# Scan of a hybrid decoder step: the samples' B and C spread over the partitions by a store and a broadcast load instead of diagonals and products with ones

## The chip, the cores and the metric

The kernel runs on one core of a Trainium2 chip. The metric is the device time of one execution in microseconds; the time before is the median of three runs. The profile is that of one execution.

## The reference, cut to what matters

One inference step of a two-layer decoder for a prompt of 1024 tokens and, beside it, 8 samples of one token each. Layer 1 is a Mamba-2 mixer with 8 groups of 4 heads (64 channels a head, 128 state elements). For the prompt it is a scan over 8 chunks of 128 tokens. For the samples, chunk length 1, it is per sample, group and head:

```
new_state = state * exp(dt * a) + outer(x * dt, B)     # (64, 128) per head
y         = new_state @ C
```

B and C are vectors of 128 elements for each sample and group. Each has to be multiplied, along the free axis, with every one of the group's 256 channels, which lie in the partitions (2 halves of 128).

## The kernel before, in words

`mamba_groups` runs the layer's input projection and the scan in one loop. All work is float32; a weight matrix comes as a high and a low part, and each product with it is made in three passes.

- In a turn of the loop (`part(g, nx)` on each engine), TensorE makes the 18 tiles of group nx = g + 1's projection (units 0 to 5 of three tiles: x, x, B, C, z, z; `tile`, line 2992) and between them, in `slot(g, k)` for k = 0 to 8, the scan of group g: `turn` (lines 3006 and 3007) turns chunk k to rows, `scan` (lines 3018 to 3026) makes the products of chunk k - 1. There is a slot behind tiles 0 to 5 and 7 to 9 of the turn. Behind slot 2 stands tile 0 of unit 1, which needs `w_low` of that unit from GpSimd (`split_low`, line 234).
- The last group has no next one. Its `closing` interleaves the slots with the first tiles of the output projection (`nxt`, class `ProjectOdd`), whose input `gated_raw` SyncE loads back from a scratch in DRAM (line 3503), ScalarE casts (line 3535) and VectorE subtracts (line 3539).
- The samples' part: GpSimd builds `dg`, the identity times the column B (later C) of each sample (`diagonals`, line 2859). TensorE multiplies it with ones (`spread`, line 3036), which leaves B of 8 samples in all partitions, in PSUM banks 6 and 7: B in slot 2, C in slot 5. VectorE multiplies from PSUM: `outer` (line 3337, behind chunk 1) and `sample_y` (line 3345, behind chunk 4).
- GpSimd, in its own order: first diagonals, six small stores of conv rows (lines 2877, 2878), then per chunk x_decayed (2922), x_d (2930), and from chunk 1 on the decay of the state (2937). In between come the decay of the sample states (2945, behind chunk 1), `w_low` of unit 1, behind chunk 3 the second diagonals and the additions to the sample states (2957), `w_low` of unit 2, and the eight stores of the sample states (2868, behind chunk 4).
- SyncE, in its own order: the spread decay sums (2 MB, line 2820), the sample states (8 loads of 128 KB, line 2826), then the weights of the units (line 220), each behind a wait for an earlier `w_low`.

Each engine runs its list strictly in order; the order is written out by hand, and engines wait for each other by semaphores that count.

Of the kernel before, what the change touches and what calls it, by code (L numbers as in the profile page):

```python
# [7 lines left out]
F32 = mybir.dt.float32  # L8
# [8 lines left out]
P = 128  # L17
# [2683 lines left out]
def mamba_groups(B, nxt, steps):  # L2701
# [29 lines left out]
    dg = B.take("diagonals_sb", [P, NS, P])  # L2731
# [13 lines left out]
    cst = gz[0:PAD + NS, 0:2, :].rearrange("p n (j c) -> p (n j) c", j=2)  # L2745
    sst = xd[:, 0, :].rearrange("p (c n) -> p c n", c=2)
    B.g_scratch = nc.dram_tensor("gated_scratch", (16, P, TOK), F32, kind="Internal").ap()
# [9 lines left out]
             "square_sums", "rstd", "gated_scaled", "gated_turned", "gated_stored_col", "diagonal", "spread", "outer",  # L2757
             "sample_state", "sample_gated", "sample_sum", "conv_rows_turned", "conv_rows_kept", "state_turned",
             "state_rows", "pad_set", "sample_scaled", "sample_decayed", "sample_mean", "column_half")
    S = {n: B.sem(n) for n in names}  # L2760
    s_bc, s_st, s_sto = B.sem("spread_loaded"), B.sem("sample_ssm_loaded"), B.sem("sample_ssm_stored")
# [37 lines left out]

    with nc.Block() as block:  # L2800
        @block.sync
        def _(sp):
# [13 lines left out]
            def part(g, nx, more):  # L2816
                if g is not None:
# [3 lines left out]
                                                ap=[[0, P], [SEQ, HPG], [1, SEQ]])).then_inc(s_bc, 16)  # L2821
                    sp.wait_ge(s_sto, g * (16 * NS))
# [5 lines left out]
                if nx is not None:  # L2828
                    for e in range(1, 6):
                        load_unit(nx, e)  # L2830
                if more:
                    load_unit(nx + 1, 0)
                if nx is None:
# [10 lines left out]
                    sp.wait_ge(S["diagonal"], G * 2)  # L2844
# [10 lines left out]
        def _(pool):  # L2855
            def diagonals(j):

                for b in range(0, NS, 4):
                    ins = nc.gpsimd.tensor_tensor(dg[:, b:b + 4], B.ident[:].unsqueeze(1).to_broadcast([P, 4, P]),
                                                  post[:, j, SEQ + b:SEQ + b + 4].unsqueeze(2).to_broadcast([P, 4, P]), ALU.mult)  # L2860
                ins.then_inc(S["diagonal"], 1)

# [39 lines left out]
            def part(g, nx, more):  # L2902
                splits = [] if nx is None else [1, 2, 3]
                if g is not None:

                    pool.wait_ge(S["conv_out"], g * 4 + 4)
                    pool.wait_ge(S["sample_gated"], g)
                    diagonals(2)
                for k in range(9):
# [7 lines left out]
                    if k < NBLK:  # L2917
# [16 lines left out]
                        if n >= 1:  # L2934
# [5 lines left out]
                                                    ALU.mult).then_inc(S["state_decayed"], 1)  # L2940
                    if k == (1 if nx is not None else 2):
# [9 lines left out]
                    if k == 3:  # L2951
# [3 lines left out]
                        diagonals(3)  # L2955
# [25 lines left out]
        def _(pe):  # L2981
# [15 lines left out]
            def turn(g, n):  # L2997

                if n == 0:
                    pe.wait_ge(S["conv_out"], g * 4 + 4)  # L3000
                    pe.wait_ge(S["gated_stored_col"], g * 8)
# [732 lines left out]
```

## Time and profile before

| what | value |
|---|---|
| median of 3 runs | 3382.21 us (3376.72 to 3386.57) |
| the profiled execution | 3382.08 us, span 3380.3 us |
| mean granted TensorE clock | 0.973 of full speed |
| TensorE busy (matmul) | 3218.8 us, 95% of the span |
| VectorE, ScalarE, GpSimd busy | 45%, 34%, 36% |
| the scan's loop with its opening and closing | about 1620 to 2490 us of the span |

In the rows below PE is TensorE, PEld its weight load, DVE VectorE, ACT ScalarE, POOL GpSimd, SP SyncE; SPq is SyncE's queue of issues. A row of the timeline gives the start and the duration in us, the engine, the line, the operation, output and inputs, and how many were merged (x4); in brackets stands the idle time of the engine ahead of it and what ended it. A granted clock of 1.00 is full speed.

### The profile page before, as it was taken

To read this page: it belongs to the slowest core of one execution; us is meant where nothing else is said; L and a number is where in the kernel's file an instruction comes from. 1 tells how busy PE (TensorE), PEld (TensorE's weight loads), DVE (VectorE), ACT (ScalarE), POOL (GpSimd) and SP (SyncE) were. 2 spreads that over 40 slices of the span, in tenths; PEclk is the share of its full clock that TensorE was granted. 3 is DMA by queue.
4 is the path that set the end of the run, shared out by engine and by line. 5 is a ranking of instruction groups with operands and counts; after the bars stand their busy time and mean duration, and the time that the engine had idled before them with its cause. 6 is when DMAs were issued, how large, how long until landed. Compare 5 with 4: busy or idle time off the path is not lost. (4 is left out here: it accounts for less than half of the span.)

```text
span 3380.3 us, 56747 instructions
## 1 busy us (share of the span) xinstructions
PE 3218.8 (95%) x20604; PEld 3043.0 (90%) x20604; DVE 1524.9 (45%) x2687; ACT 1143.0 (34%) x2132; POOL 1207.2 (36%) x890
## 2 busy tenths in 40 slices
PE   7889988889999999999999999999899999999998
PEld 6569984669999999999998899989889999999997
DVE  3699994533212212122666767776732212121222
ACT  3512214643312212133444555554532312122222
POOL 2206844413222221213356555566533121212222
PEclk9979999889999999999999999999999999999998
DMA  4218646033111111112322223321431111111111
GB/s 137 55 32 138 193 167 223 10 132 58 51 44 45 48 44 49 44 50 77 100 76 68 85 83 98 98 81 58 158 133 50 44 44 50 44 50 43 49 45 69
DMA packets 344008, 263.90 MB, mean 78 GB/s; under 512 B 52134, under 2 KB 308150, under 8 KB 341910
## 3 DMA queue, kind: packets, MB, share of 16 engines
q1 hardware_dynamic: 327926, 232.18, 23.0%
q0 software_dynamic: 8192, 19.13, 1.7%
q10 hardware_dynamic: 7776, 11.09, 1.5%
q8 instruction: 69, 1.13, 0.1%
q14 instruction: 45, 0.37, 0.0%
HBM read 219.43 MB, written 44.76 MB: 78 GB/s over the span
## 5 line engine op out<-in xcount | busy, mean ns | idle before, releaser
L234 POOL TENSOR_TENSOR w_low_sb<-w_loaded_sb,w_high_sb 128x1024 fp32r<-128x1024 f32 (+1 forms) x278 | 569.3, 2055 | 1541.0 <-ACT w_high_sb L226 1517.2
L252 PE MATMUL psum<-act_high_sb,w_high_sb 128*128 128x344 f32 (+1 forms) x2400 | 770.5, 321 | 9.5 <-PEq L2800 4.6
L252 PE MATMUL psum<-act_low_sb,w_high_sb 128*128 128x344 f32 (+1 forms) x2400 | 768.8, 320 | 0.0
L252 PE MATMUL psum<-act_high_sb,w_low_sb 128*128 128x344 f32 (+1 forms) x2400 | 768.6, 320 | 0.0
L252 PE MATMUL psum<-second_high_sb,w_high_sb 128*128 128x344 f32 x1728 | 553.3, 320 | 0.5 <-PEq L2391 0.5
L252 PE MATMUL psum<-second_low_sb,w_high_sb 128*128 128x344 f32 x1728 | 551.9, 319 | 0.0
L252 PE MATMUL psum<-second_high_sb,w_low_sb 128*128 128x344 f32 x1728 | 551.9, 319 | 0.0
L252 PEld LDWEIGHTS psum<-act_high_sb,w_high_sb 128*128 128x128 f32 (+1 forms) x2400 | 451.6, 188 | 10.3 <-issue 9.0
L252 PEld LDWEIGHTS psum<-act_low_sb,w_high_sb 128*128 128x128 f32 (+1 forms) x2400 | 451.6, 188 | 0.7 <-issue 0.3
L252 PEld LDWEIGHTS psum<-act_high_sb,w_low_sb 128*128 128x128 f32 (+1 forms) x2400 | 451.9, 188 | 0.4
L226 ACT CAST w_high_sb<-w_loaded_sb 128x1024 fp32r<-128x1024 f32 (+1 forms) x230 | 239.5, 1042 | 519.9 <-PE psum L252 498.6
L2992 PE MATMUL psum<-act_high_sb,w_high_sb 128*128 128x344 f32 x1104 | 368.4, 334 | 11.0 <-POOL w_low_sb L234 10.8
L756 DVE TENSOR_TENSOR x_sb<-x_sb,psum 128x344 f32 (+1 forms) x192 | 98.4, 513 | 600.7 <-PE psum L252 600.7
L2992 PE MATMUL psum<-act_high_sb,w_low_sb 128*128 128x344 f32 x1104 | 353.2, 320 | 0.0
L2992 PE MATMUL psum<-act_low_sb,w_high_sb 128*128 128x344 f32 x1104 | 353.0, 320 | 0.0
L252 PEld LDWEIGHTS psum<-second_high_sb,w_high_sb 128*128 128x128 f32 x1728 | 324.5, 188 | 0.8 <-issue 0.8
L252 PEld LDWEIGHTS psum<-second_high_sb,w_low_sb 128*128 128x128 f32 x1728 | 324.8, 188 | 0.0
L252 PEld LDWEIGHTS psum<-second_low_sb,w_high_sb 128*128 128x128 f32 x1728 | 324.5, 188 | 0.0
L688 ACT ACTIVATE relu_square_sb<-relu_sb 128x344 f32<-128x344 f32 x192 | 94.5, 492 | 447.0 <-DVE relu_sb L741 447.0
L741 DVE SCALAR_TENSOR_TENSOR relu_sb<-psum,rstd_sb 128x344 f32<-128x344 f32 x192 | 99.2, 517 | 293.8 <-PE psum L252 269.6
L2992 PEld LDWEIGHTS psum<-act_high_sb,w_high_sb 128*128 128x128 f32 x1104 | 208.3, 189 | 21.3 <-issue 20.1
L2992 PEld LDWEIGHTS psum<-act_low_sb,w_high_sb 128*128 128x128 f32 x1104 | 208.1, 188 | 2.6 <-issue 1.7
(434 smaller groups left out, 4758.7 us busy)
## 6 DMA issues: line engine op xcount, KB each, us to landing
w_loaded_sb<-in_w_up SPq DMA_DIRECT2D x64, 512.0 KB, 4.1
w_loaded_sb<-in_w_down SPq DMA_DIRECT2D x64, 512.0 KB, 3.6
w_loaded_sb<-in_w_in_odd SPq DMA_DIRECT2D x48, 512.0 KB, 4.0
key_pages_sb<-in_cache_k SPq DMA_DIRECT2D x64, 256.0 KB, 3.1
ecay_sum_spread_sb<-decay_sum_scratch SPq DMA_DIRECT2D x8, 2048.0 KB, 9.8
w_loaded_sb<-in_w_in_even SPq DMA_DIRECT2D x28, 512.0 KB, 4.0
value_pages_sb<-in_cache_v SPq DMA_DIRECT2D x52, 256.0 KB, 5.2
gated_scratch<-gated_sb POOLq DMA_DIRECT2D x8, 1032.0 KB, 4.4
```

What stands on the lines that cost most here:

```text
L226: self.nc.scalar.copy(self.wh[:, par, :, 0:width], self.wf[:, par, :, 0:width]).then_inc(self.s_w_high, 1)
L234: ins = self.nc.gpsimd.tensor_tensor(self.wl[:, par, k, 0:width], self.wf[:, par, k, 0:width], self.wh[:, par, k, 0:width].bitcast(F32), A ...
L252: ins = nc.tensor.matmul(out, w[:, par, k, 0:width], a[:, k, cols], start=n == 0, stop=n == 3 * KT - 1)
L688: nc.scalar.activation(self.sq[:, s, :], self.relu[:, s, :], ACT.Square).then_inc(self.s_square, 1)
L741: nc.vector.scalar_tensor_tensor(out=self.relu[:, s, :], in0=B.tile(self.par(e), t), scalar=0.0, in1=self.norm.rstd[:, tcols(t)], op0=ALU.max,
L756: nc.vector.tensor_tensor(xs, xs, B.tile(self.par(e), t), ALU.add).then_inc(B.s_tile_free, 1)
L2992: ins = nc.tensor.matmul(B.psum[:, t, 0:TT], w[:, par(e), k, :], a[:, k, tcols(t)], start=m == 0, stop=m == 3 * KT - 1)
```

## The change

The samples' B and C of a group are turned to rows by TensorE (two transposes of 8 columns, at the beginning of slot 0, into PSUM bank 6), copied to SBUF by VectorE (8 rows of 1 KB, kept in a part of the gated rows that chunk 2 uses later), stored to a scratch in DRAM by SyncE, and loaded from there to all 128 partitions by GpSimd's queue: B behind chunk 0, C behind chunk 3, each 128 times the same 8 pieces of 512 bytes. VectorE reads them from SBUF. The diagonals and the products with ones go. On SyncE the weights of units 1 and 2 now go out ahead of a wait for the rows, then the store, then the eight loads of the sample states.

```diff
-    dg = B.take("diagonals_sb", [P, NS, P])
+    spr = B.take("sample_b_or_c_sb", [P, NS, P])
...
+    bcr = gz[0:NS, 2, :].rearrange("b (i n) -> b i n", i=2)
...
+    B.bc_scratch = nc.dram_tensor("sample_b_c_scratch", (G, NS, 2, P), F32, kind="Internal").ap()
...
+    def load_spread(eng, g, i):
+
+        eng.wait_ge(s_bcs, g * 16 + 16)
+        B.hold(eng)
+        eng.dma_start(spr[:], bass.AP(tensor=B.bc_scratch.tensor, offset=g * (2 * NS * P) + i * P,
+                                      ap=[[0, P], [2 * P, NS], [1, P]])).then_inc(s_spr[i], 16)
...
# SyncE, part(g, nx), behind the load of the decay sums
+                    if nx is not None:
+                        load_unit(nx, 1)
+                        load_unit(nx, 2)
+                    sp.wait_ge(S["sample_rows"], g + 1)
+                    B.hold(sp)
+                    sp.dma_start(B.bc_scratch[bass.ds(g, 1)].rearrange("o b i n -> b (o i) n"), bcr).then_inc(s_bcs, 16)
                     sp.wait_ge(s_sto, g * (16 * NS))
                     sp.wait_ge(S["sample_gated"], g)
...
-                    for e in range(1, 6):
+                    for e in range(1 if g is None else 3, 6):
...
-                    sp.wait_ge(S["diagonal"], G * 2)
+                    sp.wait_ge(s_spr[1], 16 * G)
...
# GpSimd
-            def diagonals(j):
-
-                for b in range(0, NS, 4):
-                    ins = nc.gpsimd.tensor_tensor(dg[:, b:b + 4], B.ident[:].unsqueeze(1).to_broadcast([P, 4, P]),
-                                                  post[:, j, SEQ + b:SEQ + b + 4].unsqueeze(2).to_broadcast([P, 4, P]), ALU.mult)
-                ins.then_inc(S["diagonal"], 1)
...
-                if g is not None:
-
-                    pool.wait_ge(S["conv_out"], g * 4 + 4)
-                    pool.wait_ge(S["sample_gated"], g)
-                    diagonals(2)
...
+                    if k == 0:
+                        pool.wait_ge(S["sample_gated"], g)
+                        load_spread(pool, g, 0)
...
-                        diagonals(3)
+                        load_spread(pool, g, 1)
...
# TensorE, turn(g, 0)
+                    pe.wait_ge(S["sample_mean"], g)
+                    for i in range(2):
+                        ins = nc.tensor.transpose(B.psum[0:NS, 6, i * P:(i + 1) * P], post[:, 2 + i, SEQ:TOK], B.ident[:])
+                    ins.then_inc(S["sample_turned"], 1)
...
-            def spread(g, m):
-
-                await_group(pe, S["diagonal"], g, 2, m + 1)
-                if m == 0:
-                    pe.wait_ge(S["state_rows"], g)
-                    pe.wait_ge(S["sample_scaled"], g)
-                for a in range(2):
-                    ins = nc.tensor.matmul(B.psum[:, 6 + a, :], B.ones[:],
-                                           dg[:, 4 * a:4 * a + 4, :].rearrange("p b n -> p (b n)"), start=True, stop=True)
-                ins.then_inc(S["spread"], 1)
...
-                if k == 2:
-                    spread(g, 0)
-                if k == 5:
-                    spread(g, 1)
...
# VectorE: gate(g, 2), outer(g), sample_y(g), part(g, nx)
+                if n == 2:
+                    dve.wait_ge(s_bcs, g * 16 + 16)
...
-                await_group(dve, S["spread"], g, 2, 1)
+                dve.wait_ge(s_spr[0], g * 16 + 16)
                 for c in range(2):
-                    ins = nc.vector.tensor_tensor(tmp[:, c], B.psum[:, 6:8, :].rearrange("p a (b n) -> p (a b) n", b=4),
+                    ins = nc.vector.tensor_tensor(tmp[:, c], spr[:],
                                                   small(0)[:, c, :].unsqueeze(2).to_broadcast([P, NS, P]), ALU.mult)
...
-                await_group(dve, S["spread"], g, 2, 2)
+                dve.wait_ge(s_spr[1], g * 16 + 16)
...
+                    dve.wait_ge(S["sample_turned"], g + 1)
+                    dve.wait_ge(S["gated_turned"], g * 8)
+                    nc.vector.tensor_copy(bcr, B.psum[0:NS, 6, 0:2 * P].rearrange("b (i n) -> b i n", i=2)).then_inc(S["sample_rows"], 1)
```

## Rows read from the trace of the kernel before

**Rows 1.** Stretches view, 100 us of the loop: busy us per engine, clock, DMA
```profile
2000.00:2100.00 100.00, 96.03 (x621) 91.08 (x619) 70.60 (x110) 52.30 (x125) 56.91 (x64) 1.00 0.28 86
```

**Rows 2.** Timeline of TensorE, turn g = 1
```profile
1790.59 0.60 PE L3069 MATMUL psum<-ident_sb,conv_in_sb 128*11 128x128 f32 x4
...
1808.16 0.59 PE L3026 MATMUL psum<-x_decayed_sb,x_b_rows_sb 128*128 128x256 f32 x2
...
1808.59 1.88 PE L3036 MATMUL psum<-diagonals_sb,ones_sb 128*128 128x512 f32 x4
...
1811.51 0.42 PE L2992 MATMUL psum<-act_high_sb,w_high_sb 128*128 128x344 f32 x1 [1.04 <-POOL w_low_sb L234]
...
1831.81 0.70 PE L3026 MATMUL psum<-x_decayed_sb,x_b_rows_sb 128*128 128x256 f32 x2 [0.87 <-POOL x_decayed_sb L2922]
...
1848.46 0.38 PE L3018 MATMUL psum<-ident_sb,z_sb 128*128 128x128 f32 x2
```

**Rows 3.** Timeline, GpSimd, the same turn
```profile
1801.73 0.78 POOL L2922 TENSOR_TENSOR x_decayed_sb<-x_b_rows_sb,decay_to_end_sb 128x256 f32<-128x256 f32 x1 [0.76 <-ACT x_b_rows_sb L3186]
...
1804.20 4.07 POOL L2945 TENSOR_TENSOR ample_ssm_state_sb<-ample_ssm_state_sb,_channel_values_sb 128x512 f32<-128x512 f32 x4
...
1819.96 0.80 POOL L2937 TENSOR_TENSOR n_state_decayed_sb<-scan_state_sb,chunk_decay_sb 128x256 f32<-128x256 f32 x1
...
1820.72 2.03 POOL L2859 TENSOR_TENSOR diagonals_sb<-ident_sb,conv_out_sb 128x512 f32<-128x512 f32 x2
...
1822.72 5.65 POOL L2957 TENSOR_TENSOR ample_ssm_state_sb<-ample_ssm_state_sb,conv_sum_sb 128x512 f32<-128x512 f32 x4
```

**Rows 4.** Timeline, VectorE, the same turn
```profile
1813.42 2.36 DVE L3337 TENSOR_TENSOR conv_sum_sb<-psum,sample_small_sb 128x1024 f32<-128x1024 f32 x2
...
1827.22 1.43 DVE L3324 TENSOR_TENSOR y_sb<-y_sb,x_d_sb 128x256 f32<-128x256 f32 x1
...
1847.68 0.42 DVE L3326 TENSOR_TENSOR gated_rows_sb<-y_sb,psum 128x256 f32<-128x256 f32 x1
```

**Rows 5.** The groups by form, TensorE
```profile
L3036 PE MATMUL psum<-diagonals_sb,ones_sb 128*128 128x512 f32 x64 | 30.1, 592 | 0.0
```

**Rows 6.** Single lines (ns min/median/max) and the state loads' landing
```profile
L982 POOL DMA_DIRECT2D index_pages_sb<-in_cache_idx_k x32: 535/535/717, 83.2 to 141.9; - x32
...
L2868 POOL DMA_DIRECT2D out_ssm_sample<-ample_ssm_state_sb x64: 710/713/798, 1733.7 to 2443.1; - x64
...
L2826 SPq DMA_DIRECT2D ample_ssm_state_sb<-in_state_ssm x64: 372/446/3139, 1674.8 to 2382.4; - x64
...
DMA to landing us min/median/max: 4.0/7.1/8.5
...
L3382 DVE SCALAR_TENSOR_TENSOR conv_sum_sb<-conv_in_sb,conv_weights_sb,conv_sum_sb x96: 1283/1285/2160, 1641.8 to 2385.4; 128x1024 f32<-128x1024 f32 x96
```

**Rows 7.** TensorE's timeline at two idle times, and stretches there
```profile
615.12 1.86 PE L1898 MATMUL psum<-qkv_sb 64*128 64x512 f32 x4 [2.06 <-DVE minus_row_max_sb L1963]
...
615.40:618.80 3.40, 3.40 (x13) 1.76 (x12) 2.95 (x7) 1.03 (x2) 0.73 (x1) 0.50 0.00 0
...
571.35 1.13 PE L1898 MATMUL psum<-qkv_sb 64*128 64x512 f32 x4 [1.34 <-DVE minus_row_max_sb L1968]
...
568.00:575.00 7.00, 5.66 (x56) 3.08 (x60) 3.96 (x15) 3.52 (x8) 0.73 (x1) 1.00 0.01 2
```

**Rows 8.** Timeline of the last group's beginning, and gated_raw's landing
```profile
2387.89 4.82 SPq L3503 DMA_DIRECT2D gated_raw_sb<-gated_scratch  x8
...
2394.89 2.66 POOL L2859 TENSOR_TENSOR diagonals_sb<-ident_sb,conv_out_sb 128x512 f32<-128x512 f32 x2
...
2396.36 3.90 ACT L3535 CAST act_high_sb<-gated_raw_sb 128x1032 fp32r<-128x1032 f32 x4
...
2401.89 1.22 PE L3026 MATMUL psum<-x_decayed_sb,x_b_rows_sb 128*128 128x256 f32 x2 [2.77 <-POOL x_decayed_sb L2922]
...
DMA to landing us min/median/max: 5.3/6.9/8.7
```

More of the change, by code:

```diff
@@ L2756, in mamba_groups @@
              "exps", "cb_masked", "scores", "x_dt", "x_decayed", "x_d", "state_decayed", "state", "gated",
-             "square_sums", "rstd", "gated_scaled", "gated_turned", "gated_stored_col", "diagonal", "spread", "outer",
+             "square_sums", "rstd", "gated_scaled", "gated_turned", "gated_stored_col", "sample_turned", "sample_rows", "outer",
              "sample_state", "sample_gated", "sample_sum", "conv_rows_turned", "conv_rows_kept", "state_turned",
@@ L2760, in mamba_groups @@
     S = {n: B.sem(n) for n in names}
+    s_bcs, s_spr = B.sem("sample_b_c_stored"), [B.sem("sample_b_loaded"), B.sem("sample_c_loaded")]
     s_bc, s_st, s_sto = B.sem("spread_loaded"), B.sem("sample_ssm_loaded"), B.sem("sample_ssm_stored")
@@ L3053, in sample_sum @@
                 pe.wait_ge(S["sample_gated"], g + 1)
+                pe.wait_ge(S["sample_rows"], g + 1)
                 nc.tensor.matmul(B.psum[:, 6, 0:16], B.ones[:], sml[:, 3, :], start=True, stop=True).then_inc(S["sample_sum"], 1)
@@ L3090, in turn_state @@
                 await_group(pe, S["state"], g, NBLK, NBLK)
+                pe.wait_ge(S["state_rows"], g)
                 for j in range(2):
@@ L3341, in sample_y @@
             def sample_y(g):
-                await_group(dve, S["spread"], g, 2, 2)
+                dve.wait_ge(s_spr[1], g * 16 + 16)
                 dve.wait_ge(S["sample_state"], g + 1)
                 for c in range(2):
-                    step(nc.vector.tensor_tensor(tmp[:, c], B.psum[:, 6:8, :].rearrange("p a (b n) -> p (a b) n", b=4),
+                    step(nc.vector.tensor_tensor(tmp[:, c], spr[:],
                                                  st[:, :, c, :], ALU.mult))
```

## The prediction

> **What bounds the kernel now.** I read the busy times first: 100 us of the scan's loop hold 96.0 us of TensorE at full clock, and no other engine comes near [rows 1]. So work taken off TensorE can pay in full, 4 us in 100 are waits, and what counts is where they stand. Next came the timeline of one turn of the loop at the places where the products with ones stand, for TensorE and for GpSimd, then VectorE's, and last SyncE's order. All times are of the turn g = 1; the other six turns with a next group look alike.
>
> At the end of slot 2 TensorE makes the first spread and then still stands 1.04 us for w_low of the next unit, from GpSimd, until 1811.51. At slot 5 it stands 0.87 us for x_decayed of chunk 4, from GpSimd again, and makes the second spread behind it [rows 2]. So at both places where work is taken from TensorE, GpSimd is the later of the two. At slot 7 no wait is seen, but gated of chunk 5 ends at 1848.10 on VectorE (1847.68 + 0.42), 0.36 us ahead of the scan that needs it, L3018 at 1848.46 [rows 2, 4].
>
> **What is taken from TensorE.** A spread is four passes in 1.88 us, each of 0.59, so they follow at (1.88 - 0.59) / 3 = 0.43 us and cost 1.72 us; 16 of them (64 passes) 27.5 us [rows 2, 5]. Added are two turns of eight columns per group. The nearest row is that of the four turns of the conv rows, 0.60 us [rows 2]: 0.15 each, 0.3 us per group, 2.4 in all. Net 25.1 us, if nothing else ended the waits. The two turns are free in slot 0, as TensorE waits for the first scores in slot 1 anyway, and VectorE's copy of eight rows (0.4 us by its forms of 256 columns [rows 4]) falls in its wait for the first rows.
>
> **The GpSimd side, first half.** The first diagonals (as long as the second, 2.03 us [rows 3]) stand ahead of stores and a wait for ScalarE; nothing is won by their going. What comes in is the issue of a load of 128 x 8 pieces of 512 bytes, behind x_d of chunk 0. Its landing is hidden: it goes out near 1802 and is used at 1813.42 [rows 4], and the slowest of the state loads lands in 8.5 us [rows 6]. Its issue isn't hidden. GpSimd's issues take 0.54 us for one piece in each of 128 partitions and 0.71 for two pieces [rows 6]. By the count of pieces eight would be 0.54 + 7 x 0.17 = 1.73; if only the form counts, 0.71. I take 1.2, about the middle, as eight pieces are far from both. Of it 0.76 us fall in the wait ahead of x_decayed of chunk 1 [rows 3]; 0.44 us push the decay of the states and w_low behind it: TensorE gets w_low 0.44 us later (0 to 0.97), though it comes there 1.7 us earlier.
>
> The states of the samples are now loaded behind the rows instead of a half turn ahead. The copy is done near 1795.7 (the first chunk's turns end there), SyncE's store is issued by 1796.2, the eight loads at 0.45 us each (median of 64 issues) by 1799.8 (the last one from 1799.4 on). Behind the 2 MB load they took 4.0 us to land at the least and 7.1 in the median; now that load is long done, so I take 4.0: 1803.4 for the last. The other end is 1806.5. GpSimd wants them at 1804.20 + 0.44 [rows 3, 6]. I cost it at nothing; at the other end w_low is 1.9 us later still, and each us of it costs 7 in seven turns.
>
> **The clock.** TensorE is now done with slot 2 at 1808.75 (1808.16 + 0.59) and gets w_low at 1811.5 + 0.44: it idles 3.2 us where it idled 1.04. An idle time of 2.06 us ahead of 615.12 is followed by 3.4 us at a granted clock of 0.50, the lower of the two levels (1.2 of 2.4 GHz), with TensorE busy throughout; 1.34 us ahead of 571.35 leave it at 1.00 [rows 7]. I found no idle time of 2 us or more, entered at full clock, without such a fall. So I expect a fall in each turn, of which some 3.2 us lie in work at half rate: 1.6 us lost. Slot 3 starts 0.44 + 1.6 = 2.0 us late.
>
> **Second half of the turn.** Chunk 3 goes through all engines 2.0 us late, up to GpSimd's decay of the state at 1819.96. Then the diagonals (2.03) give way to the second issue (1.2): the additions start 2.0 - 2.03 + 1.2 = 1.2 us late [rows 3], and so do w_low, x_decayed of chunk 4 and VectorE's gate and sample_y. TensorE waits for x_decayed, then saves the spread: 1.2 - 1.7 = 0.5 us early at slot 6. But VectorE's chain from sample_y through gate 5 is 1.2 us late and a little more, as its products read SBUF on both sides instead of PSUM: 1.285 us by the nearest form, undisturbed, for 1.18 (2.36 / 2) [rows 4, 6]; I take 0.2 us for the two. Gated of chunk 5 comes at 1849.5, so TensorE, there 0.5 us early, waits 1.6 us and goes on 1.15 us late. The slack of VectorE ahead of chunk 7 gives 0.25 back by slot 8 (estimated). Rest: 0.9 us later per turn, 7 turns: +6.3 us. With an issue of 0.71 it is about 0 per turn, with 1.73 it is +2.0.
>
> A y + x_d of 256 columns takes 1.43 us at 1827.22, with GpSimd's additions (1822.72 to 1828.37) under way, and a form of as many columns with a PSUM operand 0.42 [rows 3, 4]: two SBUF inputs can be held up. The Trainium skill, page "SBUF — State Buffer", section "Who interferes with whom", has it as a rule: a VectorE instruction with two SBUF inputs contends with a GpSimd instruction that reads SBUF, and one blocks the other whole. The trace agrees. By it outer and sample_y, now with two SBUF inputs, would be open to blocks of up to one addition each (5.65 / 4 = 1.4 us), 0.9 us per turn would become up to 2.3, and the sum up to +12; I keep 0.2, since in the trace GpSimd waits during the one and issues stores during the other.
>
> **The last group.** There SyncE's order changes most: the loads of gated_raw, issued from 2387.89 on, now stand behind the wait for the sample's rows and eight state loads. The rows exist at about 2390, so gated_raw goes out from 2394.2 on, 6.3 us later (0.6 us for the store, eight loads at 0.45). Before, its landing (5.3 us at the least) left 3.2 us until the first cast at 2396.36; now the casts start about 2.5 us later. A cast is 1.0 us (3.90 / 4), the low part 1.3 by the form of 1024 columns, so the first pair is there at 2401.2. Against it, GpSimd loses 2.66 us of diagonals ahead of x_decayed of chunk 0, for which TensorE waited 2.77 us until 2401.89 [rows 6, 8]. Together TensorE opens the unit, then at 2402.55, some 1.0 us earlier, and saves two spreads (3.4 us), as other engines wait for TensorE there: -4.3 us (from -6 to +1).
>
> **Sum.** +6.3 - 4.3 = +2.0 us on the profiled execution's own 3382.1, which lies on the median of the three runs (3382.2): 3384 us.
>
> **Rivals.** (a) TensorE's work counts in full: -25.1, 3357 us. For it speaks only how busy TensorE is; against it the waits at both places. 4%. (b) The clock does not fall at slot 2 (the idle time ahead of 571.35 is its support). The turn then loses 1.6 less: additions 0.4 us early, -0.7 per turn, 7 x -0.7 - 4.3 = -9.2, 3373 us; with an issue of 0.71, -1.6 per turn, 3366 us. 20% for faster. (c) Slower: the 1.6 us for which TensorE waits at slot 7 let the clock fall a second time. It decides somewhere between 1.34 us (no fall) and 2.06 (fall) [rows 7]; each fall costs 1.6, 7 of them 11.2: 3395 us. With an issue of 1.73 as well (each 0.1 us of issue costs 1.4 us in seven turns): 3402. (d) Slower too: the state loads land at the late end, 1.9 x 7 = 13 us: 3397 us; it decides from 1806 on. (c) and (d) together 33%. (e) gated_raw comes later than worked out: up to +5 in the last group, 3389, within the forecast. The forecast with (e): 43%.
>
> A difference of 0.3%, 10 us, is about what a measurement of this kernel can tell from no change. Faster 0.24, same 0.43, slower 0.33. The likeliest case alone spans 3376 to 3392 (issue 0.71 to 1.73 with one fall); the range takes in (b), (c) and (d): 3364 to 3404 us. It leaves out (a), and (c) and (d) at once.
>
> The Trainium skill, page "DMA: Bandwidth & Descriptors", section "Anatomy of one DMA", would give the landing of 512 KB an estimated 3.2 us, hidden here too; no run here shows it yet.
>
> **What the profile after would show.** L3036 gone, two turns of 8 columns in slot 0; two GpSimd issues per group, near 1.2 us each; TensorE's wait for w_low behind slot 2 grown from 1.0 to about 3 us, with a granted clock of 0.50 behind it; the wait for x_decayed kept; a new wait of 1.6 us at L3018 of slot 7 for gated; no wait of GpSimd for the states; in the last group, later casts of gated_raw. Wrong would make it: an issue over 2 us, states that land well after 1804, a clock that stays at 1.00, or a turn in which VectorE is not the last at slot 7.

## The result, and the profile after

The kernel after takes 3427.9 us (median of four runs, 3426.35 to 3429.79) against 3381.0 us for the kernel before on the same chip: a ratio of 1.0135, 95% interval 1.0122 to 1.0148. The change makes it 47 us slower. The forecast was 3384 us, and its range ended at 3404.

First the same 100 us of the loop as in [rows 1] (columns as there):

```profile
2000.00:2100.00 100.00, 89.52 (x572) 86.62 (x570) 70.22 (x108) 47.70 (x111) 50.03 (x58) 0.95 0.29 91
```

TensorE is busy for 89.5 us instead of 96.0, and the clock's mean is 0.95. The turns of the loop show where the time is. The turn of [rows 2 to 4] lasted 99.55 us (1790.59 to 1890.14); its counterpart, from the first row below to the last, lasts 105.12. All seven grew, to between 103.4 and 108.2, 40.7 us in all. What lies ahead of them grew by 1.3 us, the last group and all behind it by 5.6.

TensorE's timeline of that turn (start, duration, in brackets the idle time and what ended it):

```profile
1797.49 0.60 PE L3066 MATMUL psum<-ident_sb,conv_in_sb 128*11 128x128 f32 x4
...
1818.43 0.42 PE L2999 MATMUL psum<-act_high_sb,w_high_sb 128*128 128x344 f32 x1 [2.79 <-POOL w_low_sb L234]
...
1841.68 0.66 PE L3029 MATMUL psum<-ident_sb,z_sb 128*128 128x128 f32 x2 [4.50 <-DVE gated_rows_sb L3326]
...
1902.61 0.60 PE L3066 MATMUL psum<-ident_sb,conv_in_sb 128*11 128x128 f32 x4
```

The first wait was forecast (3.2 us; it is 2.79). The second one, 4.50 us at the beginning of slot 5, for `gated` of chunk 3, was not. Where it comes from is seen on GpSimd and on VectorE. GpSimd:

```profile
1807.82 0.97 POOL L2807 DMA_DIRECT2D sample_b_or_c_sb<-sample_b_c_scratch  x1
...
1829.18 0.95 POOL L2807 DMA_DIRECT2D sample_b_or_c_sb<-sample_b_c_scratch  x1
1830.15 4.98 POOL L2964 TENSOR_TENSOR ample_ssm_state_sb<-ample_ssm_state_sb,conv_sum_sb 128x512 f32<-128x512 f32 x4
1835.08 2.50 POOL L234 TENSOR_TENSOR w_low_sb<-w_loaded_sb,w_high_sb 128x512 fp32r<-128x512 f32 x2
1837.55 0.60 POOL L2926 TENSOR_TENSOR x_decayed_sb<-x_b_rows_sb,decay_to_end_sb 128x256 f32<-128x256 f32 x1
1838.12 0.78 POOL L2934 TENSOR_TENSOR x_d_sb<-x_b_rows_sb,d_skip_sb 128x256 f32<-128x256 f32 x1
```

VectorE:

```profile
1831.90 6.54 DVE L3296 TENSOR_TENSOR x_dt_sb<-x_b_rows_sb,dt_rows_sb 128x256 f32<-128x256 f32 x1 [0.70 <-ACT x_b_rows_sb L3184]
1838.57 0.88 DVE L3303 TENSOR_TENSOR ecay_sum_spread_sb<-ecay_sum_spread_sb,cb_masked_sb 128x512 f32<-128x512 f32 x1
...
1841.16 0.42 DVE L3326 TENSOR_TENSOR gated_rows_sb<-y_sb,psum 128x256 f32<-128x256 f32 x1
```

At this place the kernel before had:

```profile
1823.42 0.85 DVE L3298 TENSOR_TENSOR x_dt_sb<-x_b_rows_sb,dt_rows_sb 128x256 f32<-128x256 f32 x1 [0.70 <-ACT x_b_rows_sb L3186]
```

`x_dt` of chunk 4, a product of 128 x 256 that takes 0.43 us elsewhere and 0.85 at this place before, lasts 6.54 us. It is ready to run 1.75 us behind the beginning of the additions. Behind the issue GpSimd works without a pause: four additions, two pieces of `w_low` (1.25 us each), x_decayed and x_d of chunk 4. x_dt ends at 1838.44, 0.29 us behind the end of x_decayed (1838.15), so it was let in only there, between x_decayed and x_d. GpSimd itself isn't slowed. `scores` and then `gated` of chunk 3 stand behind it in VectorE's order, TensorE waits for the latter. It is so in each of the seven turns, 6.54 to 7.42 us. The line's own row (ns minimum/median/maximum of all 64) and that of the issues:

```profile
L3296 DVE TENSOR_TENSOR x_dt_sb<-x_b_rows_sb,dt_rows_sb x64: 424/426/7417, 1700.8 to 2509.3; 128x256 f32<-128x256 f32 x64
...
L2807 POOL DMA_DIRECT2D sample_b_or_c_sb<-sample_b_c_scratch x16: 937/955/985, 1702.7 to 2474.0; - x16
```

TensorE's two falls of the clock in this turn, behind slot 2 and at slot 5 (stretch, its length, busy us of TensorE, its weight loads, VectorE, ScalarE and GpSimd, granted clock, DMA share, GB/s):

```profile
1818.40:1823.20 4.80, 4.76 (x20) 4.77 (x21) 3.88 (x5) 0.00 (x0) 1.80 (x3) 0.64 0.41 109
...
1841.68:1844.90 3.22, 3.22 (x13) 3.04 (x14) 1.41 (x3) 2.79 (x9) 3.22 (x5) 0.50 0.52 163
1844.90:1846.95 2.05, 2.05 (x8) 1.87 (x7) 0.95 (x3) 0.82 (x1) 2.03 (x4) 0.50 0.62 192
```

The second fall costs more than the first: TensorE works for 5.27 us (3.22 + 2.05) at 0.50.

The waits of TensorE, summed over the execution:

```profile
PE psum L3029 <- DVE gated_rows_sb L3326: 34.5, 8, 5.4
...
PE psum L2999 <- POOL w_low_sb L234: 23.0, 14, 2.8
```

And the last group, SyncE, ScalarE, VectorE and TensorE, for [rows 8]:

```profile
2432.70 4.11 SPq L2842 DMA_DIRECT2D ample_ssm_state_sb<-in_state_ssm  x8
2436.91 4.37 SPq L3506 DMA_DIRECT2D gated_raw_sb<-gated_scratch  x8
...
2442.86 2.00 ACT L3538 CAST act_high_sb<-gated_raw_sb 128x1032 fp32r<-128x1032 f32 x2 [4.38 <-DMA gated_raw_sb<-gated_scratch]
...
2463.12 4.01 DVE L3337 TENSOR_TENSOR conv_sum_sb<-sample_b_or_c_sb,sample_small_sb 128x1024 f32<-128x1024 f32 x2
...
2469.93 0.62 PE L3570 MATMUL psum<-act_high_sb,w_high_sb 128*128 128x344 f32 x1 [5.37 <-DVE x_sb L3583]
```

Its turn begins at 2429.67, 42.02 us later than before. The casts of gated_raw (2396.36 before) are 46.5 us later, so 4.5 us late in the turn. `outer`, 2.36 us in every other turn, takes 4.01: here it runs beside the decay of the sample states.

### The profile page after: what moved, and what is told of

The parts are those of the page before. It is cut to its first block and busy times, and to the rows that moved or that the text cites. A ratio compares the mean times of both kernels' runs of the same rounds, so it can differ in the third digit from the quotient of the medians.

```text
span 3427.9 us, 56729 instructions
## 1 busy us (share of the span) xinstructions
PE 3216.9 (94%) x20556; PEld 3057.9 (89%) x20556; DVE 1559.3 (45%) x2695; ACT 1143.3 (33%) x2132; POOL 1183.6 (35%) x874
```

## The experiments

Sixteen kernels were run. "x_dt(4)" is x_dt of chunk 4. A product is "held" where VectorE's row for it is longer than it is undisturbed; a "boundary" is the place between two GpSimd instructions that follow each other without a pause. Ratios are against the kernel before, run on the same chip, with 95% intervals; the runs were spread over several chips, so compare by the ratios.

**1. GpSimd waits for x_dt(4) ahead of the additions.** Theory A: the place within GpSimd's row of work decides. B: the load of C does. C: the clock's fall at slot 2 is the root. To kernel after:

```diff
                         load_spread(pool, g, 1)
+                        await_group(pool, S["x_dt"], g, NBLK, 5)
```

> The kernel after, in which GpSimd waits for VectorE's x_dt of chunk 4 before it begins the four additions to the sample states. Theory A (a product with two SBUF inputs is held through GpSimd's chain of additions and w_low when it comes within the chain): x_dt of chunk 4 takes 0.43 us instead of 6.54, the additions begin about 2.2 us later, x_decayed of chunk 4 is done near 2.7 us later than before and TensorE waits for it in slot 5, some 1.4 us per turn less than it waited for gated of chunk 3: about 3418 us (from 3428). Theory B (what holds x_dt is the load of C, issued by GpSimd just ahead): x_dt stays over 3 us though GpSimd stands, and the time rises by 2 us per turn, to about 3442.

3410.4 us, 1.0079 (1.0062 to 1.0096), below what either gave. x_dt(4) takes 0.43 us. GpSimd stood idle for 2.29 us while the load was landing; `scores` (4), asked for 0.04 us behind the beginning of the additions, ran at the first boundary (1.79 us). TensorE now waits 17.8 us in all for x_decayed, at most 2.5. The hold is what costs, and with idle time between issue and additions it does not come; the run does not separate A from B.

**2. Kernel before, second diagonals ahead of x_decayed(3).**

```diff
+                    if k == 3:
+                        pool.wait_ge(S["outer"], g + 1)
+                        diagonals(3)
...
-                        diagonals(3)
...
+                if m == 1:
+                    pe.wait_ge(S["outer"], g + 1)
```

> The kernel before, in which GpSimd makes the second diagonals ahead of x_decayed of chunk 3 (it stands idle there for 4 us), so that the additions begin 2.0 us earlier and x_dt of chunk 4 comes 2.7 us behind their beginning instead of 0.70. No broadcast load is in it. Theory A (place in the chain decides): x_dt of chunk 4 is now held for 3 us or more, and the turn is up to 3 us longer, up to 3400 us. Theory B (the load of C is needed for a hold): x_dt stays under 1.3 us, the wait of 0.87 us for x_decayed of chunk 4 goes, 7 x 0.87 = 6 us: 3375 us.

3377.0 us, 0.9981 (0.9971 to 0.9991). x_dt(4) comes 2.88 us behind the additions' beginning and takes 1.34 us: it gets in at the next boundary. A falls for this place.

**3. Kernel after, with the passes kept.** In slots 2 and 5 TensorE multiplies ones with twice 512 columns, as many passes as before; the result goes to PSUM banks 6 and 7 and is used by nobody.

```diff
+            def unused(g):
+                pe.wait_ge(S["sample_rows"], g + 1)
+                pe.wait_ge(S["state_rows"], g)
+                for a in range(2):
+                    nc.tensor.matmul(B.psum[:, 6 + a, :], B.ones[:], post[:, 2, a * 512:(a + 1) * 512], start=True, stop=True)
...
+                if k in (2, 5):
+                    unused(g)
```

> The kernel after with the eight passes per group of before kept on TensorE (ones times 512 columns, the result used by nobody), at the same two places, so that the clock at slot 2 stays full. Theory C (the fall of the clock at slot 2 is the root: it makes chunk 3 late and brings x_dt of chunk 4 into the chain): x_dt of chunk 4 under 1.5 us, about 3395 us. Theory A: chunk 3 and the additions are late together, so x_dt of chunk 4 is still held 5 us or more, and the time stays within 8 us of 3428.

3429.3 us, 1.0134 (1.0117 to 1.0151). The wait behind slot 2 is 1.07 us again, x_dt(4) takes 6.54 to 7.42 us as in the kernel after, TensorE waits 32.4 us for gated (34.5). C falls. It also shows that the 25 us of passes taken off TensorE are worth nothing here: with or without them the time is the same.

**4. The loads issued by SyncE** (in the seven turns; the last group's stay on GpSimd).

```diff
 # SyncE, behind the loads of the sample states
+                    if nx is not None:
+                        load_spread(sp, g, 0)
...
                         load_unit(nx, e)
+                        if e == 3 and g is not None:
+                            sp.wait_ge(S["outer"], g + 1)
+                            load_spread(sp, g, 1)
 # GpSimd
-                    if k == 0:
+                    if k == 0 and nx is None:
...
+                        if nx is None:
+                            load_spread(pool, g, 1)
```

> The kernel after with the broadcast loads of the seven turns issued by SyncE (B behind the states of the samples, C behind the weights of unit 3) instead of GpSimd. Theory A: GpSimd is 0.95 us earlier at w_low of unit 1 and again at the additions; x_dt of chunk 4 comes deeper in the chain and is held until its end, which is 0.95 us earlier: 5.5 us instead of 6.5. The wait behind slot 2 falls to 1.8 us, where the clock may or may not fall. 2 to 3.5 us per turn less: 3404 to 3414 us. Theory B: with no load issued by GpSimd the hold is gone, x_dt under 1.3 us: 3375 to 3390 us.

3380.5 us, 0.9993 (0.9982 to 1.0003). The whole loss is gone, as B had it. The additions and x_dt(4) in its profile:

```profile
1819.68 5.17 POOL L2973 TENSOR_TENSOR ample_ssm_state_sb<-ample_ssm_state_sb,conv_sum_sb 128x512 f32<-128x512 f32 x4
...
1822.39 1.32 DVE L3305 TENSOR_TENSOR x_dt_sb<-x_b_rows_sb,dt_rows_sb 128x256 f32<-128x256 f32 x1 [0.70 <-ACT x_b_rows_sb L3193]
```

TensorE's wait behind slot 2 is 2.74 us, and a turn lasts 98.85 us.

**5 and 6. Place against load.** A product of 128 x 512 by ones on GpSimd (result unused) ahead of the additions: in 5 added to the kernel of run 4, in 6 to the kernel after, between issue and additions.

```diff
+                        pool.wait_ge(s_gout, g * 16)
+                        nc.gpsimd.tensor_tensor(gst[:, 0, 0:512].rearrange("p (b n) -> p b n", b=4), post[:, 2, 0:512].rearrange("p (b n) -> p b n", b=4),
+                                                B.ones[:].unsqueeze(1).to_broadcast([P, 4, P]), ALU.mult)
                         for b in range(0, NS, 2):
```

> The kernel with the loads issued by SyncE (the fourth run), plus one product of 128x512 by ones on GpSimd ahead of the additions, whose result nobody uses (about 1.0 us, as long as the issue that it stands in for). x_dt of chunk 4 comes then 1.7 us behind the additions' beginning, as in the kernel after (1.75), but no load goes out or lands there. Theory A (the place within the chain decides): x_dt is held through the chain again, over 5 us, and the time rises to 3405 us or more. Theory B (the load issued by GpSimd, or its landing, is needed): x_dt stays under 1.5 us, and the time rises by at most 7 us, to 3382 to 3388.

3391.8 us, 1.0028 (1.0017 to 1.0038). x_dt(4) comes 1.46 us behind the beginning and takes 1.32: let in at the next boundary. The time is 4 us above B's range: a turn lasts 100.4 us on average, 1.6 more than in run 4, for a product of 1.28 us.

> The kernel after plus the same product on GpSimd between the issue of C's load and the additions: the load is still issued by GpSimd and lands during the additions, but x_dt of chunk 4 comes 0.7 us behind their beginning, as in the kernel before. Theory A (place): x_dt ends at the first boundary, under 1.5 us; the time falls by some 20 us or more in spite of 1.0 us of added work per turn, to about 3400. Theory B (load): x_dt is held until the chain's end, 7.5 us or more, and the time rises by up to 7 us, to 3435.

3440.7 us, 1.0169 (1.0152 to 1.0186). The rows of GpSimd and VectorE:

```profile
1830.60 0.95 POOL L2807 DMA_DIRECT2D sample_b_or_c_sb<-sample_b_c_scratch  x1
1831.57 1.28 POOL L2964 TENSOR_TENSOR gated_sb<-conv_out_sb,ones_sb 128x512 f32<-128x512 f32 x1
1832.80 5.01 POOL L2967 TENSOR_TENSOR ample_ssm_state_sb<-ample_ssm_state_sb,conv_sum_sb 128x512 f32<-128x512 f32 x4
...
1833.32 7.79 DVE L3299 TENSOR_TENSOR x_dt_sb<-x_b_rows_sb,dt_rows_sb 128x256 f32<-128x256 f32 x1 [0.70 <-ACT x_b_rows_sb L3187]
```

x_dt(4) comes 0.52 us behind the additions' beginning, where the kernel before let it in at the next boundary, and is held for 7.79 us. The time is 6 us above B's. Both runs speak for B and against A.

**7. Run 4 with w_low of unit 1 ahead of x_decayed(0) on GpSimd.**

```diff
-                    if splits and k % 2 == 0 and k > 0:
+                    if splits and k % 2 == 0 and k > 0 and not (k == 2 and g is not None):
...
                         store_conv_rows(g)
+                        if splits:
+                            e = splits.pop(0)
+                            B.split_low(pool, unit(nx, e), par(e), pieces=2)
```

> The fourth run's kernel with w_low of unit 1 made on GpSimd ahead of x_decayed of chunk 0, where GpSimd stands idle for 2.7 us, instead of behind the decay of the sample states. If TensorE's wait behind slot 2 (2.7 us) and the half clock behind it (1.6 us) are the rest of the loss, both go: 7 x 4.3 = 30 us, 3350 us. If VectorE or the sample states' loads are the next bound at slot 2 or 3, the gain is under 12 us: 3368 or more.

3364.4 us, 0.9943 (0.9926 to 0.9959). The wait behind slot 2 and the half clock there are gone; a turn lasts 96.1 us, two of the seven 97.7. The gain is 16 us, not 30: what is left are waits in slot 5 for x_decayed (0.87 us) and in slot 7 (1.55), and behind the latter the clock falls in the two long turns (mean 0.66 from 1940 to 1944) and stays at 1.00 in the others looked at (1841.6 to 1846).

**8. Run 2 with the same move of w_low.**

> The kernel before with both moves on GpSimd: the second diagonals ahead of x_decayed of chunk 3 (the second run) and w_low of unit 1 ahead of x_decayed of chunk 0. The wait of 1.0 us for w_low behind slot 2 goes, 7 us less than the second run's 3377: 3370 us. But GpSimd's idle time there is only 1.2 us with the diagonals ahead of it, so x_decayed of chunk 0 comes 1.3 us later; if that is passed on, the gain is nothing: 3377.

3377.3 us, 0.9982 (0.9972 to 0.9991): no gain over run 2. The two moves help the new form of the kernel and hardly the old one.

**9 and 10. Issue against landing.** 9: run 4, and GpSimd issues at the old place a copy of the same pieces within DRAM, read by nobody. 10: run 4, and SyncE issues C's load only when the additions begin.

```diff
 # 9, GpSimd, ahead of the additions
+                        if nx is not None:
+                            B.hold(pool)
+                            pool.dma_start(copied[bass.ds(g, 1)].rearrange("o p b n -> (o p) b n"),
+                                           bass.AP(tensor=B.bc_scratch.tensor, offset=g * (2 * NS * P) + P,
+                                                   ap=[[0, P], [2 * P, NS], [1, P]])).then_inc(s_cpy, 16)
 # 10, SyncE
                             sp.wait_ge(S["outer"], g + 1)
+                            await_group(sp, S["state_decayed"], g, NBLK - 1, 3)
                             load_spread(sp, g, 1)
```

> The kernel with the loads issued by SyncE (the fourth run), in which GpSimd issues, where C's load was issued in the kernel after, a copy of the same 128 x 8 pieces of 512 bytes from DRAM to DRAM that nobody reads: GpSimd's issue is there, and nothing is written to SBUF by it. Theory B1 (the issue by GpSimd is enough): x_dt of chunk 4, which comes 1.75 us behind the beginning of the additions, is held for 6.5 us, and the time goes to 3405 us or more. Theory B2 (the landing in SBUF is needed): x_dt stays under 1.5 us, and the time is that of the fifth run, 3385 to 3395.

3427.6 us, 1.0134 (1.0118 to 1.0151): the time of the kernel after, with nothing landing in SBUF.

```profile
1828.95 0.86 POOL L2976 DMA_DIRECT2D copied_scratch<-sample_b_c_scratch  x1
1829.79 5.01 POOL L2980 TENSOR_TENSOR ample_ssm_state_sb<-ample_ssm_state_sb,conv_sum_sb 128x512 f32<-128x512 f32 x4
...
1831.67 6.44 DVE L3313 TENSOR_TENSOR x_dt_sb<-x_b_rows_sb,dt_rows_sb 128x256 f32<-128x256 f32 x1 [0.70 <-ACT x_b_rows_sb L3201]
```

> The kernel with the loads issued by SyncE, in which SyncE lets C's load out only when GpSimd has decayed the state of chunk 3, so that it lands in all partitions while GpSimd makes the additions and x_dt of chunk 4 is asked for. Theory B1 (the issue by GpSimd is what matters): x_dt stays at 1.3 us and the time within 4 us of the fourth run's 3380. Theory B2 (the landing): x_dt is held for 5 us or more, 3405 us or more.

3381.2 us, 1.0003 (0.9994 to 1.0013). The load goes out at 1818.01 and the DMA engines are busy with it from 1819.1 to 1821.5; x_dt(4), asked for at 1820.44, takes 1.32 us. So it is GpSimd's issue, not the landing.

**11. Run 7 with gated_raw's loads ahead of the wait for the sample's rows** (last group).

```diff
+                    else:
+                        sp.wait_ge(s_gout, 16 * (KT // 2))
+                        sp.wait_ge(B.s_tile, first_next * 3 + 6)
+                        nxt.load_raw(sp)
                     sp.wait_ge(S["sample_rows"], g + 1)
```

> The seventh run's kernel (loads by SyncE, w_low of unit 1 early), in which in the last group SyncE lets out the loads of gated_raw ahead of its wait for the sample's rows, as in the kernel before. If those loads' lateness (4.5 us at the casts) is the cost of the last group, TensorE's waits there (3.4 and 5.6 us) shrink, and the time falls by 3 to 5 us, to 3360. If outer, now with two SBUF inputs beside the decay of the sample states (4.01 us for 2.35), decides, it falls by under 1.5 us: 3363.

3361.3 us, 0.9940 (0.9923 to 0.9956). Against run 7's 0.9943 that is no difference that the times can tell. In the traces the next stage begins 107.8 us behind the last turn's start instead of 111.5, but the execution ends only 0.5 us sooner. Inconclusive.

**12. Run 11 with the additions ahead of x_decayed(3).**

```diff
+                    if k == 3 and nx is not None:
+                        pool.wait_ge(S["outer"], g + 1)
+                        pool.wait_ge(S["sample_decayed"], g + 1)
+                        additions()
                     if k < NBLK:
```

> The kernel of the run before this one, in which GpSimd makes the additions to the sample states of the seven turns ahead of x_decayed of chunk 3, where it stands idle for about 5 us, instead of behind chunk 3: they and w_low of unit 2 no longer follow each other, and x_decayed of chunk 4, for which TensorE waits 0.9 us per turn, is early. 7 x 0.9 = 6 us less, 3354 us. If x_decayed and x_d of chunk 3, which then come some 4 us later, hold up TensorE or VectorE in slot 4, it is not faster: 3360 or more.

3387.0 us, 1.0016 (1.0007 to 1.0026): slower than run 11 by 26. VectorE comes to `sample_y` 0.3 us ahead of the end of GpSimd's eight store issues, and its two products take 6.6 us (2.78 in run 4), the first of them 4.4, through x_decayed, x_d, the decay and a piece of w_low. In the first turn it is y + x_d that comes there, and it is held for 4.55 us. TensorE waits 2.57 to 2.65 us for gated in each turn. It looks like the same hold, behind another issue.

**13. The kernel after with C's issue ahead of x_decayed(3).**

```diff
+                    if k == 3 and nx is not None:
+                        pool.wait_ge(S["outer"], g + 1)
+                        load_spread(pool, g, 1)
                     if k < NBLK:
...
-                        load_spread(pool, g, 1)
+                        if nx is None:
+                            load_spread(pool, g, 1)
```

> The kernel after, in which GpSimd issues C's load of the seven turns ahead of x_decayed of chunk 3, where it then stands idle until chunk 3's rows are there, instead of just ahead of the additions. If the hold needs an issue without idle time between it and the chain: x_dt of chunk 4 takes 1.3 us as in the fourth run, and only B's issue on GpSimd (0.97 us at slot 2) stands between the two: 3380 + 7 = 3387 us. If an issue some microseconds ahead is enough: x_dt stays held for 5 us or more, 3420 us or more.

3382.5 us, 0.9999 (0.9988 to 1.0009). One instruction in another place takes away 45 us of the 47.

```profile
1812.28 0.94 POOL L2807 DMA_DIRECT2D sample_b_or_c_sb<-sample_b_c_scratch  x1 [3.34 <-DVE conv_sum_sb L3341]
1814.46 0.78 POOL L2929 TENSOR_TENSOR x_decayed_sb<-x_b_rows_sb,decay_to_end_sb 128x256 f32<-128x256 f32 x1 [1.24 <-ACT x_b_rows_sb L3188]
...
1817.94 5.17 POOL L2968 TENSOR_TENSOR ample_ssm_state_sb<-ample_ssm_state_sb,conv_sum_sb 128x512 f32<-128x512 f32 x4
...
1820.64 1.32 DVE L3300 TENSOR_TENSOR x_dt_sb<-x_b_rows_sb,dt_rows_sb 128x256 f32<-128x256 f32 x1 [0.70 <-ACT x_b_rows_sb L3188]
```

**14. Run 9 with 128 pieces instead of 1024.** The copy's access pattern is [[0, P], [1, P]] on the side of the source.

> The ninth run's kernel (a copy in DRAM issued by GpSimd just ahead of the additions), with 128 pieces of 512 bytes instead of 1024. If the number of pieces makes the hold: x_dt under 1.5 us and 3380 to 3388 us. If any issue does: x_dt is held until the end of w_low, 6 us or more, and the time is 3415 us or more. Its issue is shorter (about 0.5 us), so x_dt comes some 2.2 us behind the additions' beginning.

3423.1 us, 1.0119 (1.0102 to 1.0135). The issue takes 0.59 us, x_dt(4) comes 2.12 us behind the additions' beginning and is held for 5.73 us, to the end of w_low, in two of the seven turns; in the other five it is held for 6.75 us, to the end of x_d of chunk 4. The hold does not need the 1024 pieces.

**15. Run 11 with the stores of the sample states issued by SyncE** (in the seven turns, behind the weights of unit 4).

```diff
+                        if e == 4 and g is not None:
+                            out_states(sp, g, s_sto)
...
-                    if k == 4:
-                        out_states(g)
+                    if k == 4 and nx is None:
+                        out_states(pool, g, s_stol)
```

> The eleventh run's kernel, in which the eight stores of the sample states of the seven turns are issued by SyncE too, behind the weights of unit 4. GpSimd has 5.8 us less per turn and no issue left in the second half: y + x_d and x_decayed behind the stores come when they are ready, and no product with two SBUF inputs is held for more than 1.5 us in slots 5 to 7. TensorE's wait of 1.6 us in slot 7 (for VectorE, in its slot 6) goes in part: 2 us or less per turn, 3350 to 3361 us. If w_low of unit 3, now 5 us earlier, falls on sample_y and holds it up, nothing is won: 3361.

3352.2 us, 0.9909 (0.9892 to 0.9925): faster than both kernels. TensorE's wait in slot 7 is 0.80 us (1.55). sample_y takes 3.98 us, its products being let in at boundaries of w_low.

**16. The kernel after with both moves, and all issues on GpSimd** (13 and the move of 7).

> The kernel after with both loads still issued by GpSimd, but C's ahead of x_decayed of chunk 3 and w_low of unit 1 made ahead of x_decayed of chunk 0. If the two places explain the loss, it lies near the seventh run (3364), plus up to 1 us per turn for B's issue, now ahead of work that nobody waits for: 3364 to 3371 us. If an issue by GpSimd costs more than its place, it is 3385 or more.

3371.2 us, 0.9969 (0.9957 to 0.9982), the upper end of what the two places were to give. In the profile six of the seven turns last 96.0 to 96.1 us, as in run 7, but the fourth lasts 105.4:

```profile
2005.48 0.94 POOL L2807 DMA_DIRECT2D sample_b_or_c_sb<-sample_b_c_scratch  x1 [5.61 <-issue]
2006.44 0.63 POOL L2932 TENSOR_TENSOR x_decayed_sb<-x_b_rows_sb,decay_to_end_sb 128x256 f32<-128x256 f32 x1
...
2013.03 2.47 POOL L234 TENSOR_TENSOR w_low_sb<-w_loaded_sb,w_high_sb 128x512 fp32r<-128x512 f32 x2
...
2006.93 8.86 DVE L3331 TENSOR_TENSOR y_sb<-y_sb,x_d_sb 128x256 f32<-128x256 f32 x1
```

There C's issue went out 1.1 us later in the turn than in the turn before, why is not shown, and GpSimd found its work ready: x_decayed, x_d, the decay, the additions and w_low follow without a pause. y + x_d, asked for 0.51 us behind the issue's end, is held to the end of w_low, and TensorE stands idle for 8.37 us. The hold is back, behind an issue that had been moved.

The cases side by side, all in the second turn of the trace (for run 1 it is `scores` that was asked for in the additions; "their" is the additions'):

| kernel | GpSimd's issue ahead of the additions | GpSimd idle between | asked for behind their beginning | took |
|---|---|---|---|---|
| after | 1024 pieces to SBUF | no | 1.75 us | 6.54 us |
| 3 | 1024 pieces to SBUF | no | 1.75 | 6.56 |
| 6 | 1024 pieces to SBUF, then a product | no | 0.52 | 7.79 |
| 9 | 1024 pieces in DRAM | no | 1.88 | 6.44 |
| 14 | 128 pieces in DRAM | no | 2.12 | 5.73 |
| 1 | 1024 pieces to SBUF | 2.29 us | 0.04 | 1.79 |
| 13 | 1024 pieces, 4.7 us ahead | 1.24 and 1.37 us | 2.70 | 1.32 |
| 4, 10 | none (10: SyncE's load lands) | | 2.71 | 1.32 |
| 5 | none | | 1.46 | 1.32 |
| 2 | none | | 2.88 | 1.34 |

## Why the prediction was wrong

**Right.** That the passes taken off TensorE gain nothing at slots 2 and 5 (run 3: kept, they cost nothing). The issue of the broadcast load: 0.955 us in the median for 1.2, within 0.71 to 1.73. The landing of B and of the states: hidden, GpSimd does not wait for either, so rival (d) did not come; from issue to landing the loads of B and C took 4.9 us in the median (4.6 to 8.2), against the estimate of 3.2. The wait behind slot 2: 2.79 us for 3.2. The clock's fall behind it, but in five of the seven turns (0.50 for 3.4 us each); behind the waits of 2.78 us at 1923.55 and 2.73 at 2347.13 it stays at 1.00. "A fall in each turn" was too much, and [rows 7] did not carry it. Chunk 3 is asked for 1.57 us later in the turn than before (cb_masked at 1824.60 - 1797.49 against 1816.13 - 1790.59) for 2.0. Runs 4 and 7 price the wait with the falls: without them 16 us less.

**The step that failed** is in the second half of the turn: "its products read SBUF on both sides instead of PSUM ... I take 0.2 us for the two", with blocks of up to one addition each as the other end, +12 us in all. Two things were wrong in it. It looked at the products that the change gives a second SBUF input, and not at those that had two all along and now meet another GpSimd. And it took a block to end at the next boundary of GpSimd's instructions, as [rows 4] show (1.43 us). The runs show that behind an issue by GpSimd, with no idle time in between, it does not end there: x_dt(4) is held through the rest of the additions, both pieces of w_low and x_decayed of chunk 4, 6.54 us. The issue was costed by its 0.96 us alone.

**How 6 us of hold become the 47.** In the turn shown gated of chunk 3 is ready at 1841.58; TensorE waits 4.50 us for it, and behind the wait 5.27 us of its work run at 0.50, which costs another 2.6 us. That is rival (c)'s mechanism, in slot 5 and behind another wait. Run 13 is the same kernel without the hold: its second turn lasts 98.89 us, with a wait of 0.97 us at this place. 4.50 - 0.97 + 2.6 = 6.2 us (an estimate from these rows), and 6.2 us lie between the two turns (105.12 and 98.89). Seven turns grew by 40.7 us where +6.3 was forecast. Run 13 as a whole is at 3382.5, so that the hold and what follows from it cost 45 us.

In slot 7, where rival (c) stood, TensorE waited 1.2 to 2.1 us in five of the seven turns (forecast: 1.6), but for another reason than forecast: they are the turns in which y + x_d behind the issues of the eight stores took 2.8 to 4.4 us. Once, behind 2.09 us at 2283.04, the clock fell there too; that turn is the longest, 108.2 us. Without the hold, in runs 4 and 13, no wait over 0.6 us comes at slot 7, and the turn is 98.9 us, 0.7 less than before, where 0.9 more was forecast. That the additions would be 1.2 us late was too much as well (0.5 in the turn shown of the kernel after).

The Trainium skill, page "SBUF — State Buffer", section "Who interferes with whom", says that a VectorE instruction with two SBUF inputs contends with a GpSimd instruction that reads SBUF, and that the pair of ports they share is an exclusive lock for which the order of issue decides. By it a wait would end with the GpSimd instruction under way. Runs 2, 4, 5, 10 and 13 agree (1.32 to 1.34 us, one boundary). The kernel after and runs 3, 6, 9 and 14 do not: there the wait goes on over four to seven boundaries, and in the one turn of run 16 over eight. The measurement decides. The Trainium skill, same page, section "Summary: rules for kernel authors", advises issuing a DMA from ScalarE's or SyncE's queue, for another reason, that VectorE can keep GpSimd from writing its descriptors; run 4 issues from SyncE and wins 47 us.

**The last group.** Forecast were -4.3 us; the stretch from its turn's start to the end of the execution grew by 5.6 (992.65 to 998.2). That is one execution of each kernel: in runs 4, 7 and 13, whose last group is the same as the kernel after's, the stretch took 994.4, 994.8 and 998.9. Up to the next stage alone the turn took 106.3 us before and 112.6 after, and the mean granted clock of its first 130 us fell from 0.92 to 0.88. Three of its terms can be read. The casts of gated_raw are 4.5 us late for 2.5; the prediction's own terms, 6.3 us later at the issue less 3.2 us of room, give 3.1 and not 2.5. TensorE opens the unit 15.65 us behind the turn's start for 14.9 before: 0.75 late instead of 1.0 early. And the two spreads saved turned into a wait, as in the turns: 5.37 us at 2469.93 for x_sb, 0.96 before (2424.15). Outer, now with two SBUF inputs and beside the decay of the sample states, takes 4.01 us for 2.35, which is 1.7 of those 4.4 us at most; where the rest comes from is not shown. What the late casts are worth stays open: run 11 puts the loads first and comes to the next stage 3.7 us sooner in its trace than run 7, but its time can't be told from run 7's.

**Open.** Why an issue by GpSimd makes its following instructions keep VectorE out, and what ends the hold: it ended behind x_decayed in the turn shown, behind w_low or behind x_d in run 14, each time at a boundary like those passed over. And it does not always come: B's issue at 1807.82 is followed by x_decayed and x_d without a pause, and `scores` of chunk 1, asked for 0.28 us behind it, took 0.93 us; behind the eight stores y + x_d took between 1.5 and 4.4 us in the seven turns; in run 8 w_low and x_decayed follow the six small stores of conv rows without a pause, and an x_dt asked for 1.1 to 1.2 us behind the last of them took 1.7 us in five turns. Nor is the idle time separated from the distance: the x_dt(4) that were held were asked for 0.6 to 2.1 us behind the end of C's issue or of the copy, the products that were let in at the next boundary 2.3 us (`scores` in run 1) and 7.4 us (run 13) behind it. A product asked for 3 us or more behind an issue, with GpSimd busy without a pause, would tell the two apart; it was not run. Which of these conditions decides is not shown.

## What to carry to other kernels

The price of an issue on GpSimd is not its duration: ask what GpSimd does next without a pause, and which VectorE instruction with two SBUF inputs is asked for during it, above all one that the change does not touch. Issue from SyncE, or put the issue where GpSimd goes idle afterwards; here that was worth 45 of 47 us. The second cure is the weaker one: in run 16 an issue that came 1.1 us later than in the turn before it found no idle time behind it, and that turn took 9.3 us more. Work taken off the busiest engine is worth nothing where that engine waits for another next, and a wait of 1.5 us or more can bring a stretch of half clock with it.

## What the runs showed of the hardware that was not expected

- Behind an issue by GpSimd a VectorE product of two SBUF inputs was held over five to nine GpSimd instructions, 5.7 to 8.9 us (after, runs 3, 6, 9, 14, and one turn of run 16), whether the issue had 1024 or 128 pieces and whether it wrote to SBUF or to DRAM. A load from SyncE's queue landing at the same time did nothing (run 10).
- The issue of the load of 128 x 8 pieces took GpSimd 0.94 to 0.99 us. As a copy within DRAM it took 0.85 to 0.88 us, and 0.58 to 0.60 with 128 pieces (runs 9 and 14), so about 0.04 us for each further piece per partition. The SyncE issue of the same load took 0.37 us.
- Waits of one length did not always move TensorE's clock in one way: behind 2.76 us at 2133.59 it fell, behind 2.78 at 1923.55 it did not, and in run 7 it fell behind one of 1.55 us at 1937.69 and not behind one of 1.57 at 1841.56. A fall behind 1.55 us cost 1.6 us, as turns with and without it show (97.7 and 96.1 in run 7). Behind the longer wait of 4.50 us 5.27 us of work were at half rate, 2.6 us lost.
